# Both gate/up stages: 18 of 22 weight units as 2 x 2 blocks with seven half-sized products in place of eight

## The reference

```python
h = rms_norm(x, norm_ffn_pre)
f = (silu(h @ w_gate) * (h @ w_up)) @ w_down      # 1024 -> 2816 -> 1024
```

## Time and profile before

| | |
|---|---|
| median of 3 runs | 1337.88 us (1337.88 to 1338.05) |
| span of the profiled execution | 1336.2 us, first to last instruction |
| time around the span, against the median | 1.7 us |
| TensorE busy | 1321.8 us, 99% |
| TensorE weight loads busy | 1062.0 us, 79% |
| VectorE busy | 657.8 us, 49% |
| ScalarE busy | 537.7 us, 40% |
| first gate/up stage, first matmul of it to first down matmul | about 237 to 477 us |
| second gate/up stage | about 918 to 1158 us |

### The profile page before, as it was taken

One profiled execution on the slowest core, in us unless ns is written; L12 is line 12 of the kernel. 1 busy time (PEld: TensorE's weight loads), 2 busy tenths in 40 slices (PEclk: granted clock), 3 DMA queues, 4 the chain that ended last, 5 costly groups with the idle time before them and its releaser, 6 DMA issues.

```text
span 1336.2 us, 14846 instructions
## 1 busy us (share of the span) xinstructions
PE 1321.8 (99%) x6184; PEld 1062.0 (79%) x6184; DVE 657.8 (49%) x907; ACT 537.7 (40%) x732; POOL 93.4 (7%) x95
## 2 busy tenths in 40 slices
PE   9999999999999999999999999999999999999998
PEld 7864568788888888887888888888888888888887
DVE  4887663755353531227434555563644443423246
ACT  6568654533232322234225556533423232322235
POOL 0000004300000000003000001011000000000103
PEclk9999999999999999999999999999999999999999
DMA  7200013122222223242221111222222222223321
GB/s 300 107 32 1 1 63 127 64 95 95 95 95 95 85 87 108 87 136 75 101 95 63 64 63 64 94 95 95 95 95 95 95 95 95 82 91 96 109 95 64
DMA packets 21170, 119.85 MB, mean 90 GB/s; under 512 B 2544, under 2 KB 2928, under 8 KB 10480
## 3 DMA queue, kind: packets, MB, share of 16 engines
q1 hardware_dynamic: 20400, 118.20, 25.3%
q10 hardware_dynamic: 704, 0.70, 0.2%
HBM read 116.80 MB, written 2.10 MB: 89 GB/s over the span
## 4 chain that ended last, share of the span: by engine, by line
PE 94%; DVE 3%; ACT 1%; DMA 1%; issue 1%; SPq 0%; DVEq 0%; ACTq 0%
PE ps L504 92%; PE ps L751 2%; DMA w_raw<-weights 1%; DVE w_lo L1445 1%; DVE prob L1449 0%; ACT prob L995 0%; DVE nmax L1663 0%; ACT w_hi L995 0%; DVE rt L1452 0%; DVE hf L1452 0%; SPq L443 0%; PE ps L585 0%; SPq L439 0%; DVE X L1445 0%; DVE h_lo L1445 0%
## 5 line engine op out<-in xcount | busy, mean ns | idle before, releaser
L504 PE MATMUL ps<-h_hi,w_hi 128*128 128x512 f32 (+1 forms) x1256 | 491.8, 392 | 1.6 <-DVE w_lo L1445 0.9
L504 PE MATMUL ps<-h_hi,w_lo 128*128 128x512 f32 (+1 forms) x1256 | 487.4, 388 | 0.0
L504 PE MATMUL ps<-h_lo,w_hi 128*128 128x512 f32 (+1 forms) x1256 | 487.4, 388 | 0.0
L1445 DVE TENSOR_TENSOR w_lo<-w_raw,w_hi 128x2048 fp32r<-128x2048 f32 (+2 forms) x117 | 240.9, 2062 | 273.2 <-ACT w_hi L995 273.2
L995 ACT ACTIVATE w_hi<-w_raw 128x2048 fp32r<-128x2048 f32 (+2 forms) x117 | 201.3, 1722 | 201.2 <-DMA w_raw<-weights 201.1
L504 PEld LDWEIGHTS ps<-h_hi,w_hi 128*128 128x128 f32 x1256 | 235.8, 188 | 56.8 <-issue 6.1
L504 PEld LDWEIGHTS ps<-h_hi,w_lo 128*128 128x128 f32 x1256 | 235.8, 188 | 48.7
L504 PEld LDWEIGHTS ps<-h_lo,w_hi 128*128 128x128 f32 x1256 | 235.9, 188 | 48.6 <-issue 1.0
L504 PE MATMUL ps<-mid_hi,w_hi 128*128 128x512 f32 x352 | 136.9, 389 | 0.0
L504 PE MATMUL ps<-mid_lo,w_hi 128*128 128x512 f32 x352 | 136.9, 389 | 0.0
L504 PE MATMUL ps<-mid_hi,w_lo 128*128 128x512 f32 x352 | 136.9, 389 | 0.0
(11 more groups left out here) (193 smaller groups left out, 1097.0 us busy)
## 6 DMA issues: line engine op xcount, KB each, us to landing
w_raw<-weights SPq DMA_DIRECT2D x81, 1024.0 KB, 4.9
w_raw<-weights SPq DMA_DIRECT2D x32, 704.0 KB, 4.2
PT<-x SPq DMA_DIRECT2D x4, 512.0 KB, 15.8
out<-OUT SPq DMA_DIRECT2D x8, 256.0 KB, 2.5
X<-x_t SPq DMA_DIRECT2D x3, 512.0 KB, 7.1
c<-constants SPq DMA_DIRECT2D x1, 1280.0 KB, 11.8
w_raw<-weights SPq DMA_DIRECT2D x4, 256.0 KB, 6.8
wp_raw<-weights SPq DMA_DIRECT2D x1, 1024.0 KB, 6.9
```

The source lines that it names most:

```text
L504: return nc.tensor.matmul(out, lhsT, rhs, start=start, stop=stop, skip_group_check=loose)
L1445: return nc.vector.tensor_tensor(out, a, b, op)
```

## The change

Units 0 to 3 of each stage stay as they are. The other 18 are computed as 2 x 2 blocks: the depth of 1024 in two halves of 4 tiles, the 256 output channels in the unit's two chunks, and the 512 tokens in two halves of 256. Eight block products per unit would be 4 x 3 matmuls of 256 columns each; by Strassen's scheme in Winograd's form it is seven products of sums of blocks.

- The activation side is prepared once a stage. `normed` writes x times gain times factor (so h is now complete, and no factor is needed on evacuation); `op_difference` makes four sums, and seven operands B11, T1, T2, T3, B21, B22, T4 of 4 tiles x 256 columns are split high and low (`op_high` on ScalarE, `op_low` on VectorE).
- The weight side is prepared for each unit: VectorE makes four sums of blocks (`sums`, `last_sum`), one of them in place in `w_raw`; four blocks (`base_*`) and three further ones (`extra_*`) are split.
- TensorE's `halved_units`: the products B11 and T1 of a unit (`lead`) go to bank 4 or 5 and are issued ahead, in the middle of the unit before. ScalarE copies B11's result into the two output banks (`seed`), on which T2 and T3 accumulate, and T1's result to SBUF. VectorE adds this to the accumulated half at two points (`blend`). B21, B22 and T4 accumulate onto the rest.
- Silu reads the gate's banks directly; VectorE's product reads the up's banks and `sq` and writes a mid tile as float32.
- These mid tiles are split into `mid_hi` and `mid_lo` only when the gate/up products are through, with 22 instructions on each of the two engines, beside the first down chunk.
- Tiles are laid out anew in SBUF; the final gate reads `g_hi`, `g_lo` in place of `h_hi`, `h_lo`.

The core of the diff (indentation shortened by 8):

```diff
+HALF = S // 2
+BLOCK = 4 * P
+PLAIN_UNITS = 4
+SPLIT_UNITS = UNITS_FF - PLAIN_UNITS
+B11, T1, T2, T3, B21, B22, T4 = range(7)
...
+        if phase in ("ff1", "ff2") and j >= 2 * PLAIN_UNITS and j % 4 < 2:
+            e = "S"
...
+    def block_product(bank, whi, wlo, o, start=False):
+        for k in range(4):
+            t = slice(k * P, (k + 1) * P)
+            mm(bank, whi[:, t], ops_r[:, o, 0, k, :], start and k == 0, False, loose=True)
+            mm(bank, whi[:, t], ops_r[:, o, 1, k, :], False, False, loose=True)
+            last = mm(bank, wlo[:, t], ops_r[:, o, 0, k, :], False, k == 3, loose=True)
+        return last
...
+    def operand(v, o, n):
+        if v == 0:
+            pe.wait_ge(op_lo, 7 * n + o + 1)
+    def lead(v, u, n):
+        pe.wait_ge(lead_lo, SPLIT_UNITS * n + v + 1)
+        if v >= 2:
+            pe.wait_ge(five_ready, SPLIT_UNITS * n + v - 1)
+        bank = ps[:, 4 + v % 2, :]
+        operand(v, B11, n)
+        block_product(bank[:, 0:HALF], *base_block(u, 0), B11, start=True)
+        operand(v, T1, n)
+        block_product(bank[:, HALF:S], *base_block(u, 2), T1).then_inc(lead_done, 1)
+    def halved_units(phase, u_ff, n):
+        u0, c0 = u_ff + PLAIN_UNITS, SPLIT_UNITS * n
+        lead(0, u0, n)
+        for v in range(SPLIT_UNITS):
+            u, c = u0 + v, c0 + v
+            first, second = ps[:, 2 * (v % 2), :], ps[:, 2 * (v % 2) + 1, :]
+            pe.wait_ge(seeded, c + 1)
+            pe.wait_ge(extra_lo, 3 * c + 1)
+            operand(v, T2, n)
+            block_product(second[:, 0:HALF], *extra_block(v, 0), T2).then_inc(mixed, 1)
+            if v + 1 < SPLIT_UNITS:
+                lead(v + 1, u + 1, n)
+            pe.wait_ge(blended, 2 * c + 1)
+            pe.wait_ge(extra_lo, 3 * c + 2)
+            operand(v, T3, n)
+            block_product(second[:, 0:HALF], *extra_block(v, 1), T3).then_inc(mixed, 1)
+            pe.wait_ge(lo_ready, u)
+            operand(v, B21, n)
+            block_product(first[:, 0:HALF], *base_block(u, 1), B21)
+            pe.wait_ge(extra_lo, 3 * c + 3)
+            operand(v, B22, n)
+            block_product(first[:, HALF:S], *extra_block(v, 2), B22).then_inc(group_done, 1)
+            pe.wait_ge(blended, 2 * c + 2)
+            operand(v, T4, n)
+            block_product(second[:, 0:HALF], *base_block(u, 3), T4).then_inc(group_done, 1)
...
-        for u in range(2, UNITS_FF):
+        for u in range(2, PLAIN_UNITS):
             unit(phase, u_ff + u, 2 * u, 2, KS, h_hi, h_lo)
+        halved_units(phase, u_ff, mids0 // KF)
 
         for j in range(KD):
             wait_bank(down, j)
             for part in range(2):
                 u = u_down + 2 * j + part
                 pe.wait_ge(lo_ready, u)
-                group(u % SLOTS, 0, range(part * DOWN_TILES, (part + 1) * DOWN_TILES), j % 2, mid_hi, mid_lo,
-                      part == 0, part == 1, (prod_lo, mids0) if j == 0 else None)
+                last = None
+                for t, k in enumerate(range(part * DOWN_TILES, (part + 1) * DOWN_TILES)):
+                    if j == 0:
+                        pe.wait_ge(prod_lo, mids0 + k + 1)
+                    last = three(j % 2, u % SLOTS, t, mid_hi[:, k, :], mid_low(k), k == 0, k == KF - 1)
+                last.then_inc(group_done, 1)
...
+        def op_high(o):
+            act.wait_ge(op_ready, 6 * n + (1, 4, 5, 3, 2, 2, 6)[o])
+            af(ops_r[:, o, 0, :, :], ops[:, o, 1, :, :], ACT.Copy).then_inc(op_hi, 1)
+        def base_high(v, part):
+            act.wait_ge(sums_ready, 4 * (c0 + v) + 2)
+            af(base_pair(w_hi, u0 + v, part), base_pair(w_raw, u0 + v, part), ACT.Copy
+               ).then_inc(hi_ready if part else lead_hi, 1)
+        def extra_hi_one(v, i):
+            act.wait_ge(sums_ready, 4 * (c0 + v) + (3, 1, 4)[i])
+            af(extra_high(v, i), extra_full(v, i), ACT.Copy).then_inc(extra_hi, 1)
+        def seed(v):
+            p = v % 2
+            act.wait_ge(lead_done, c0 + v + 1)
+            if v == 0:
+                act.wait_ge(evac_dve, EVAC[phase, 2 * PLAIN_UNITS - 3][1])
+            elif p:
+                act.wait_ge(evac_dve, EVAC[phase, 2 * (PLAIN_UNITS + v) - 3][1])
+            else:
+                act.wait_ge(silu_ready, EVAC[phase, 2 * (PLAIN_UNITS + v) - 3][1])
+            af(ps[:, 2 * p:2 * p + 2, 0:HALF],
+               ps[:, 4 + p, 0:HALF].unsqueeze(1).to_broadcast([P, 2, HALF]), ACT.Copy).then_inc(seeded, 1)
...
+        op_high(B11)
+        silu_plain(0)
+        split(u_ff + 3)
+        op_high(T1)
+        base_high(0, 0)
+        op_high(T2)
+        extra_hi_one(0, 0)
+        op_high(T3)
+        extra_hi_one(0, 1)
+        base_high(0, 1)
+        op_high(B21)
+        extra_hi_one(0, 2)
+        op_high(B22)
+        op_high(T4)
+        base_high(1, 0)
+        seed(0)
+        silu_plain(1)
+        extra_hi_one(1, 0)
+        extra_hi_one(1, 1)
+        base_high(1, 1)
+        extra_hi_one(1, 2)
+        for v in range(SPLIT_UNITS):
+            if v % 2:
+                silu_halved(v - 1)
+            if v + 1 < SPLIT_UNITS:
+                seed(v + 1)
+            if v + 2 < SPLIT_UNITS:
+                base_high(v + 2, 0)
+                extra_hi_one(v + 2, 0)
+                extra_hi_one(v + 2, 1)
+                base_high(v + 2, 1)
+                extra_hi_one(v + 2, 2)
+            else:
+                split(u_down + v + 2 - SPLIT_UNITS)
+        for k in range(KF):
+            mid_high(k)
...
+        def normed(k):
+            o, step = (B11, T1 - B11) if k < 4 else (B21, B22 - B21)
+            halves = "p (h c) -> p h c"
+            ins = stt(ops[:, o:o + step + 1:step, 1, k % 4, :], X[:, k, :].rearrange(halves, h=2),
+                      gcol(name, k), factors_sb[:, :].rearrange(halves, h=2), ALU.mult, ALU.mult)
+            if k % 4 == 3:
+                ins.then_inc(op_ready, 1)
+        def op_difference(o, a, b, op, count):
+            dve.wait_ge(op_ready, 6 * n + count)
+            tt(ops[:, o, 1, :, :], ops[:, a, 1, :, :], ops[:, b, 1, :, :], op).then_inc(op_ready, 1)
+        def op_low(o):
+            dve.wait_ge(op_hi, 7 * n + o + 1)
+            low(ops_r[:, o, 1, :, :], ops[:, o, 1, :, :], ops_r[:, o, 0, :, :]).then_inc(op_lo, 1)
...
+        def sums(v):
+            c = c0 + v
+            dve.wait_ge(*landed(u0 + v))
+            if v >= 2:
+                dve.wait_ge(mixed, 2 * (c - 2) + 2)
+            tt(extra_full(v, 1), raw_block(v, 2), raw_block(v, 0), ALU.subtract).then_inc(sums_ready, 1)
+            dve.wait_ge(sums_ready, 4 * c + 1)
+            tt(raw_block(v, 2), raw_block(v, 2), raw_block(v, 3), ALU.subtract).then_inc(sums_ready, 1)
+            dve.wait_ge(sums_ready, 4 * c + 2)
+            tt(extra_full(v, 0), raw_block(v, 0), raw_block(v, 2), ALU.subtract).then_inc(sums_ready, 1)
+        def last_sum(v):
+            c = c0 + v
+            dve.wait_ge(sums_ready, 4 * c + 3)
+            if v >= 2:
+                dve.wait_ge(group_done, GROUP[phase, 2 * (PLAIN_UNITS + v - 2)])
+            tt(extra_full(v, 2), raw_block(v, 1), extra_full(v, 0), ALU.subtract).then_inc(sums_ready, 1)
+        def base_low(v, part):
+            u = u0 + v
+            dve.wait_ge(sums_ready, 4 * (c0 + v) + 3 + part)
+            dve.wait_ge(*((hi_ready, u) if part else (lead_hi, c0 + v + 1)))
+            low(base_pair(w_lo, u, part), base_pair(w_raw, u, part), base_pair(w_hi, u, part)
+                ).then_inc(lo_ready if part else lead_lo, 1)
+        def extra_lo_one(v, i):
+            dve.wait_ge(extra_hi, 3 * (c0 + v) + i + 1)
+            low(extra_low(v, i), extra_full(v, i), extra_high(v, i)).then_inc(extra_lo, 1)
+        def blend(v, part):
+            p = v % 2
+            dve.wait_ge(mixed, 2 * (c0 + v) + part + 1)
+            dve.wait_ge(five_ready, c0 + v + 1)
+            tt(ps[:, 2 * p + part, HALF:S], ps[:, 2 * p + 1, 0:HALF], fives(v), ALU.add
+               ).then_inc(blended, 1)
+        def up_halved(v):
+            j = 2 * (PLAIN_UNITS + v)
             for c in range(2):
+                dve.wait_ge(group_done, GROUP[phase, j + c])
+                dve.wait_ge(silu_ready, EVAC[phase, j - 2 + c][1])
+                if v == SPLIT_UNITS - 1:
+                    dve.wait_ge(blended, 2 * (c0 + v) + 2)
+                tt(mid(PLAIN_UNITS + v - 1 + c), ps[:, 2 + c, :], sq[:, c, :], ALU.mult).then_inc(evac_dve, 1)
...
+        wide_factors(nm)
+        if not wide:
+            split(u_ff + 2)
+        for k in range(KD):
+            normed(k)
+        gate_plain(0)
+        up_plain(0)
+        split(u_ff + 3)
+        op_difference(T3, B22, T1, ALU.add, 2)
+        op_difference(T1, T1, B11, ALU.subtract, 3)
+        op_difference(T2, B22, T1, ALU.add, 4)
+        op_difference(T4, B21, T2, ALU.subtract, 5)
+        sums(0)
+        last_sum(0)
+        dve.wait_ge(op_ready, 6 * n + 6)
+        op_low(B11)
+        op_low(T1)
+        base_low(0, 0)
```

(97 more changed lines are left out.)

95 lines of the change are left out of this document (59 added, 36 removed).

## The result

The changed kernel takes 1342.16 us (median of 6 runs, 1340.53 to 1342.97), the kernel before, run beside it, 1337.88 (6 runs, 1337.62 to 1338.22). The ratio is 1.0031, with a 95% interval of 1.0021 to 1.0042: slower by 4.3 us. The profiled execution took 1342.85 us, with a span of 1341.1.

The account below looks back on a forecast made before the run. TensorE was taken to bound the kernel: -28.7 (units) + 15.0 and + 12.2 (stage beginnings) + 4.0 (clock) + 2.7 (ends) = +5.2 us on 1337.88, forecast 1343.1 us, range 1337 to 1350.

Parts of the forecast that it names:

- What a unit costs: TensorE, new units: 84 matmuls at 0.1200 us, 10.08 instead of 10.88 us; 36 units give -28.7 us.
- Fulfilled waits: TensorE waits already fulfilled, at 6 boundaries in each of 36 units: 0 taken, possible 0 to +17 us.
- The rival of boundaries: Each of 216 boundaries costs TensorE 0.08 us: 1360.4 us; chance 0.10, a mid-stage slip of like size included.
- The middle: Mid-stage, VectorE needs about 8.1 of 10.08 us a unit; the first blend holds by 0.7 us; cost 0.
- The list: VectorE's serial work before the first T2 of each stage: 37.2 us; TensorE waits total 15.0 and 12.2 us.
- The waits for units 3 and 2: TensorE waits 2.5 us before unit 3 in the first stage and 5.0 before unit 2 in the second.
- the 0.9 us before the lead: First stage: the lead wants its low parts at 284.1 and gets them at 285.0, a 0.9 us wait.
- two T2 waits: TensorE idle before the first T2 product of each stage: 11.6 us in the first, 7.2 in the second.
- The clock: Idle before the first T2 of each stage lowers TensorE's granted clock: 2.0 us each, +4.0 in all.
- The ends: End of each stage: last blend's wait 0.7 us, plus mid-tile splitting delays; 1.35 a stage, +2.7 in all.
- The cover suffices: Rival: plain units cover VectorE's list before T2, so no waits or clock cost: 1311.9 us; chance 0.12.
- Idle without a fall of the clock: Rival: idle before T2 doesn't lower the clock, the tail hidden too: 1338.4 us, no change; chance 0.18.

Follow-up runs that it names:

- e_ballast1: Changed kernel with one useless VectorE addition of 512 columns (0.60 us) at the end of each unit's list in mid-stage: 1342.48 us.
- e_warm: Changed kernel with 72 (stage 1) and 36 (stage 2) extra, unread matmuls between the lead and the first T2: 1339.21 us.
- e_early_order: Changed kernel with norm products (half in stage 1, all in stage 2) moved behind what units 2 and 3 want: 1342.25 us, ratio 1.0033.
- e_ballast2: Changed kernel with two useless VectorE additions of 512 columns (1.2 us) at the end of each unit's list in mid-stage: 1352.88 us.
- e_six_early: Changed kernel with six plain units a stage instead of four, and norm products moved behind what units 2 and 3 want: 1317.31 us, ratio 0.9847.
- e_six: Changed kernel with six plain units a stage instead of four, the head of VectorE's list left as it is: 1328.00 us, ratio 0.9924.
- e_gate_up: Changed kernel with the second plain gate moved forward in VectorE's list, and ScalarE's copy of the lead with it: 1335.23 us, ratio 0.9982.
- e_longer: Changed kernel with two useless additions of 1024 columns in VectorE's list before the first T2: 1346.25 us.

## Why the prediction was right, by its steps

**What a unit costs: right.** The forecast's 84 x 0.1200 is what the trace shows. The 17 units from the first T2 at 298.83 to the last at 472.70 take 173.87 us; 17 x 10.08 is 171.4, and the other 2.5 are the slow clock at their beginning. The 109.2 ns for 256 columns that the Trainium skill's formula for the isolated gap gives ("TensorE: Matmul & The Clock Gate", section Back-to-back issue gap) is not met in any series here; by its two figures the 36 units would have saved 14 us more than they did, an estimate.

**Fulfilled waits: right, at 0.** Six and more waits per unit leave products 2.88 us apart. The rival of boundaries (+17) is out.

**The middle: right.** VectorE of the changed kernel, by the same window as above:

```profile
320.00:400.00 80.00, 80.00 (x669) 80.00 (x669) 65.18 (x96) 39.49 (x65) 0.00 (x0) 1.00 0.31 106
```

65.18 of 80 is 81%; the forecast had 8.1 of 10.08 us. Its slack of 0.7 us in every second unit is there too. VectorE's timeline has the blend for the T3 of 466.94 end 0.74 ahead of it:

```profile
465.78 0.42 DVE L1659 TENSOR_TENSOR ps<-ps,mid_back 128x256 f32<-128x256 f32 x1
```

**The list: right in place, a little long.** 36.4 us against 37.2. (The forecast rounded up on its way: 261.54 + 37.2 is 298.7 and not 298.9.) The four dependent sums of 1024 columns took 5.00 and not 5.3 (a step of 1.26, not the 1.33 I took), and the dependent sums of 512 a step of 0.72 instead of 0.79, which was a step behind an instruction that reads PSUM. The wait before T2 in stage 1 was 10.0 us from the last lead matmul's due end, against 11.6; in stage 2 4.8 against 7.2. The waits for units 3 and 2 are 2.4 and 5.0, as forecast (2.5 and 5.0).

**Not there: the 0.9 us before the lead, and part of the two T2 waits.** The forecast let TensorE run at full clock behind the first idle times. It did not: unit 3 of stage 1 took 12.6 us instead of 10.9 (four matmuls in the window 274 to 275 instead of six), and stage 2 lost 1.6 us in the same way. A slower TensorE reaches a fixed date later, so these 3.4 us came out of the waits behind them and cost nothing by themselves. e_ballast1 shows it, as its kernel is the same up to there. Behind the same idle time of 2.26 us before unit 3 its clock did not fall (windows of TensorE and timeline):

```profile
274.00:275.00 1.00, 1.00 (x6) 1.00 0.98 410
```

```profile
298.70 2.93 PE L570 MATMUL ps<-ops_r,extra_r 128*128 128x256 f32 x12 [11.27 <-ACT ps L1127]
```

Its T2 starts 61.6 us after the start of the stage, as in the changed kernel, and only the idle time before it is longer, 11.27 for 9.84. Its lead starts 0.2 us behind its due, so of the 0.9 most was the list's part ahead of the lead, which I had too long.

**The clock: the mis-sized term.** I put 2.0 us for each of two gaps and nothing for the shorter ones. There were four falls, worth 1.8, 2.5, 1.6 and 2.8 us (the last: 7.12 from T2 to T3 of stage 2, where 4.32 is full speed), together 8.7. 5.3 of them are paid (those behind T2, of which e_warm shows that of stage 2); 3.4 are taken out of the waits. The first stage in sum: 2.4 + 1.8 + 10.0 + 2.5 = 16.7 against 17.0 forecast; the second 5.0 + 1.6 + 4.8 + 2.8 = 14.2 against 14.2. So the total is near partly because the terms aren't free: whatever TensorE loses before the end of the list, the wait for the list gives back. e_early_order shows the same with the 7.4 us of idle that it takes from units 3 and 2.

That 4.0 was near 5.3 is in part luck. The nearest row that I took, the warm-up with its 421 ns, stands in a stretch where the profile of the kernel before has a granted clock of 1.00 (in every window from 1 to 8 us), so it was no measure of the slow clock. And the price isn't fixed: with the same order of work, the falls behind T2 cost from 1.6 us (e_ballast2, stage 2) to 2.8.

**The ends: right.** From the last T2 to the first down matmul of stage 1 it is 7.98 us, where five products take 7.2: 0.8, with 0.53 of it idle before the last T3. The down part grew by 0.5. Together 1.3 against 1.35.

**The rivals.** The cover suffices: out, until e_six_early makes it so. Idle without a fall of the clock: out by the windows for the long waits before T2, and e_warm at 1339.21 is near its 1338.4 only because it fills the gap; for the 2.3 us before unit 3 it is what five of the seven traces show that have this idle time. Not shown are the clock's 2.5 us of stage 1 with the gap filled to the end, what decides whether the clock falls behind 2.3 us of idle, and whether another number of plain units beats six.

## What to carry to other kernels

Before arithmetic is taken from the busy engine, lay out what the helping engine has to do before the first piece of the new kind can start, and hold its length against the time that the old kind of work covers: an average of 47% busy said nothing on 36 us of serial work due in 23. While the list is the bound, moving its items only moves the wait, and idle time or a slow clock ahead of its end is free; first give it cover (more units of the old kind), and only then does the order pay. A saving per unit of 7% on matmuls of half the width, instead of the eighth that the operation count promises, leaves little to pay for such a start.

## What was not expected of the hardware

- An idle time of 2.3 us can be followed by the fall of the clock to 1.2 GHz: in the changed kernel TensorE stops at 271, and the window from 274 is at 0.50, after TensorE had started again. It need not be: the same idle time before unit 3 (2.25 to 2.27 us) was followed by a fall in the changed kernel and in e_six, and by none in e_gate_up, e_warm, e_longer, e_ballast1 and e_ballast2 (windows from 273 to 278 at 1.00). Idle times of 0.5 to 1.0 us never did it (0.82 in e_gate_up: its T2 series takes 1.70 us, as at full clock; 1.02 in e_longer).
- The slow stretch after a restart lasted 3 to 6 us in the changed kernel (273.7 to 277; 298.83 to about 304.4; 980.83 to about 987), which costs a little less than half of that: at 0.50 the matmuls of 256 columns start 0.213 us apart (984.19 to 984.83 is three), at 1.00 0.120.
- A wait that holds TensorE by a little costs more than its idle time: 0.62 us of delay for 0.36 shown, when the data came some 0.5 us late. A fulfilled one costs nothing even at 0.120 us a matmul.
- VectorE's sums that wait for the one before follow at 0.72 (512 columns) and 1.26 us (1024), independent ones at 0.60 and 1.13.
